# A new order for the second group of an MLP projection: three products ahead of the sums, and the sums left to VectorE

## What is computed

```python
def sqrelu_mlp(u, w1, w2):
    return jnp.square(jax.nn.relu(u @ w1)) @ w2

h = h + sliding_window_attention(rmsnorm(h, mix_norm_g), ...)
h = h + sqrelu_mlp(rmsnorm(h, mlp_norm_g), m_w1, m_w2)
gate = jax.nn.sigmoid(rmsnorm(h, ple_norm_g) @ ple_w_gate)
h = h + gate * (p @ ple_w_proj)
```

## Time and profile before

| | |
|---|---|
| median of 3 runs | 1142.06 us (1140.66 to 1142.89) |
| the profiled execution | 1143.35 us |
| its span on the core | 1141.6 us |
| PE busy | 1107.6 us, 97% of the span |
| DVE busy | 765.5 us, 67% |
| ACT busy | 453.7 us, 40% |
| POOL busy | 252.9 us, 22% |

### The profile page before, as it was taken

One profiled execution on the slowest core, in us unless ns is written; L12 is line 12 of the kernel. 1 busy time (PEld: TensorE's weight loads), 2 busy tenths in 40 slices (PEclk: granted clock), 3 DMA queues, 4 the chain that ended last, 5 costly groups with the idle time before them and its releaser, 6 DMA issues.

```text
span 1141.6 us, 15063 instructions
## 1 busy us (share of the span) xinstructions
PE 1107.6 (97%) x5418; PEld 930.1 (81%) x5418; DVE 765.5 (67%) x1129; ACT 453.7 (40%) x796; POOL 252.9 (22%) x230
## 2 busy tenths in 40 slices
PE   7899999998999996999999999999999999999998
PEld 6788888886888885888888888888888888888887
DVE  5788887888553588766766676668777774564321
ACT  5565666566432314233223323553333332243100
POOL 6532322323100185324532450000000000010000
PEclk9999999999999998999999999999999999999999
DMA  7000000013142404332533234899888882111211
GB/s 277 20 19 20 18 18 18 18 34 151 38 153 87 148 19 166 148 145 114 203 148 144 115 133 144 340 408 345 286 293 289 291 287 77 38 37 56 84 40 44
DMA packets 61801, 154.41 MB, mean 135 GB/s; under 512 B 5040, under 2 KB 6064, under 8 KB 61744
## 3 DMA queue, kind: packets, MB, share of 16 engines
q1 hardware_dynamic: 61600, 153.12, 37.4%
q10 hardware_dynamic: 144, 0.52, 0.1%
HBM read 119.55 MB, written 34.08 MB: 135 GB/s over the span
## 4 chain that ended last, share of the span: by engine, by line
PE 80%; DVE 10%; POOL 3%; ACT 3%; issue 3%; DMA 0%; ACTq 0%; DVEq 0%; POOLq 0%
PE pair L1997 23%; PE pair L1976 23%; PE pair L2040 8%; PE pair L1859 6%; PE pair L1731 5%; PE pair L2017 4%; ACT probs L895 2%; PE pair L1799 2%; PE pair L2053 2%; PE pair L1770 2%; DVE probs L1298 2%; DVE probs L1316 1%; PE pair L1936 1%; PE pair L1906 1%; PE pair L1782 1%
## 5 line engine op out<-in xcount | busy, mean ns | idle before, releaser
L1997 PE MATMUL pair<-uT 128*128 128x512 f32 x1176 | 266.7, 389 | 0.0
L1997 PEld LDWEIGHTS pair<-uT 128*128 128x128 f32 x1176 | 220.7, 188 | 45.8
L1126 ACT ACTIVATE uT<-wo_raw 128x1024 fp32r<-128x1024 f32 x63 | 63.9, 1053 | 105.0 <-PE pair L1997 89.4
L638 POOL TENSOR_SCALAR row_var<-row_ssq 128x1 f32<-128x1 f32 x24 | 4.6, 192 | 437.0 <-ACT hn L1023 430.3
L1572 DVE TENSOR_TENSOR uT<-wo_raw,uT 128x1024 fp32r<-128x1024 f32 x63 | 74.8, 1221 | 39.5 <-ACT uT L1126 39.5
L1731 PE MATMUL pair<-WA,xT 128*128 128x512 f32 x384 | 96.4, 401 | 1.4 <-DVE kn L1255 1.0
L1859 PE MATMUL pair<-WA,oT 128*128 128x512 f32 x384 | 91.6, 396 | 2.3 <-DVE WA L1374 1.7
L1859 PEld LDWEIGHTS pair<-WA,oT 128*128 128x128 f32 x384 | 72.4, 191 | 17.6 <-issue 1.9
L1731 PEld LDWEIGHTS pair<-WA,xT 128*128 128x128 f32 x384 | 70.7, 191 | 17.4 <-issue 2.9
L895 ACT ACTIVATE probs<-probs,nmax 128x257 f32<-128x257 f32 x128 | 63.7, 500 | 52.3 <-DVE nmax L1303 52.1
L1976 PE MATMUL pair<-WA,WB 128*128 128x512 f32 x312 | 74.4, 396 | 3.6 <-ACT xr L1101 3.6
(11 more groups left out here) (182 smaller groups left out, 2074.7 us busy)
## 6 DMA issues: line engine op xcount, KB each, us to landing
wo_raw<-in_m_w SPq DMA_DIRECT2D x53, 512.0 KB, 6.5
wo_raw<-hid_kept SPq DMA_DIRECT2D x36, 512.0 KB, 4.6
hid_kept<-RES SPq DMA_DIRECT2D x28, 512.0 KB, 2.6
emb<-in_m_w SPq DMA_DIRECT2D x20, 512.0 KB, 6.5
RES<-in_m_w SPq DMA_DIRECT2D x8, 1024.0 KB, 6.7
RES<-in_a_wqkv SPq DMA_DIRECT2D x12, 512.0 KB, 8.8
uT_f<-in_m_w SPq DMA_DIRECT2D x6, 1024.0 KB, 6.7
act_buf<-hid_kept SPq DMA_DIRECT2D x11, 512.0 KB, 4.6
```

The costliest lines, as they stand in the source:

```text
L1126: nc.scalar.activation(operand(t, which, HI), unit(t, which), ACT.Copy).then_inc(op_hi, 1)
L1997: mm = nc.tensor.matmul(ps[4 * (j % 2) + m][:], operand(t, 0, s)[:, k, m * P:(m + 1) * P], operand(t, 1, r)[:, k, :], start=(g == 0 and k ...
```

## The change

In group 1 alone the products now stand in the order 0, 5, 3, 1, 2, 4, 6 (`FIRST_ORDER`). The first three have quadrants of `uT` as right operands. Product 3 opens a chain of its own in `pair[3]`, so z12 is joined from two places, by two additions (`z12_part`). DVE forms all four T sums; POOL no longer forms any. Three S sums of group 1, the left operand of product 3 among them, are formed in group 0 in buffers of other tensors (`early_sums`); S1 and S2 are formed again later, in their usual places. POOL's joins of group 0 have a new order, m2, m6, m5, m1, m7, and wait for the early sums. ACT splits a left operand before it takes a partial sum in group 1, and splits T3 and T4 behind the copy of z11.

```diff
+FIRST_ORDER = (0, 5, 3, 1, 2, 4, 6)
...
         def group_of(q):
-            return q // N1 + 1, q % N1
+            return q // N1 + 1, FIRST_ORDER[q] if q < N1 else q % N1
...
+        def joined_after(q):
+            g, i = group_of(q)
+            if g == 1:
+                return {5: ("z11", 1), 2: ("z12", 2), 4: ("z22", 3), 6: ("z21", 4)}.get(i, (None, 0))
+            return {3: ("z12", 1), 4: ("z22", 2), 5: ("z11", 3), 6: ("z21", 4)}.get(i, (None, 0))
...
-            pool.wait_ge(wo_half, 2 * NB)
-            pool.wait_ge(uT_ready, 2 * NB)
-            pool.tensor_tensor(WA_f[:, T4, HI], u(LO, 0, 1), u(LO, 0, 0), ALU.subtract).then_inc(t_low, 1)
-            pool.tensor_tensor(tsum[T3], u(LO, 1, 1), u(LO, 0, 1), ALU.subtract).then_inc(t3_step, 1)
-            pool.wait_ge(t3_step, 1)
-            pool.tensor_tensor(tsum[T3], tsum[T3], u(HI, 1, 1), ALU.add).then_inc(t3_step, 1)
-            pool.wait_ge(t3_step, 2)
-            pool.tensor_tensor(tsum[T3], tsum[T3], u(HI, 0, 1), ALU.subtract).then_inc(t3_step, 1)
...
-            pool.wait_ge(z_squared, 4)
-            pool.wait_ge(hn_ready, NB)
-            join("m5", 0)
             pool.wait_ge(z_squared, 8)
-            pool.wait_ge(row_moved[7], row_kept(7))
-            join("m1", 0)
-            pool.wait_ge(uT_done, 2 * NB)
+            pool.wait_ge(a_sum, summed_by(1, 3))
             join("m2", 0)
             join("m6", 0)
+            join("m5", 0)
+
+            pool.wait_ge(a_ready, 3)
+            join("m1", 0)
             join("m7", 0)
...
             for q in range(NP):
+                if q < N1:
+                    a_hi_part(q + 2)
                 if q > 0:
                     take(q - 1)
-                if q == 0:
-                    t_hi_part(T4)
+                if N1 <= q < NP - 2:
+                    a_hi_part(q + 2)
                 if q == 1:
                     t_hi_part(T3)
-                if q + 2 < NP:
-                    a_hi_part(q + 2)
+                    t_hi_part(T4)
...
                 if i == 2:
                     t1_first()
+                    t1_second()
                 if i == 3:
-                    t1_second()
+                    t1_third()
                     t2_first()
                 if i == 4:
                     t2_second()
                     t_lo_part(T1)
                 if i == 5:
-                    a_sum_part(1)
-                    t4_first()
+                    early_sums()
                 if i == 6:
                     a_lo_part(0)
+                    a_lo_part(1)
+                    t3_first()
+                if i == 7:
+                    t4_first()
                     t_lo_part(T2)
-            a_sum_part(2)
-            a_lo_part(1)
-            t4_second()
             for q in range(NP):
                 if q > 0:
                     join_chains(q - 1)
...
                 if q == 0:
-                    a_sum_part(3)
-                    t_lo_part(T4)
+                    a_sum_part(1, 1)
+                    a_sum_part(1, 2)
+                    t3_second()
+                    t4_second()
                 if q == 1:
                     t_lo_part(T3)
+                    a_sum_part(1, 4)
+                if q == 1:
+                    t_lo_part(T4)
...
-                if i in (2, 3, 4):
+                if i in (2, 4) or (i == 3 and g > 1):
                     pe.wait_ge(z_copied, 3 * (g - 1) + i - 1)
...
                 if i == 6:
-                    pe.wait_ge(z_added, 3 * (g - 1) + 2)
-                chain = {1: pair[0], 3: pair[0], 5: pair[1]}.get(i, pair[2 if g % 2 == 1 else 3])
+                    pe.wait_ge(z_added, 3 * (g - 1) + (3 if g == 1 else 2))
+                chain = {1: pair[0], 3: pair[3] if g == 1 else pair[0], 5: pair[1]}.get(i, pair[2 if g % 2 == 1 else 3])
```

More of the change, by code:

```diff
@@ L226, in a_source @@
         def a_source(g, i):
-            sums = (first_sum if g == 1 else sum_a, sum_b, sum_a, sum_b)
+            sums = (sum_a, sum_b, early_s4, sum_c) if g == 1 else (sum_a, sum_b, sum_a, sum_b)
             return {0: lambda: w1_quadrant(g, 0, 0), 1: lambda: sums[0], 2: lambda: sums[1], 3: lambda: sums[2],
@@ L531, in _ @@
             sp.wait_ge(z_ready, 8)
-            sp.wait_ge(t_step, 1)
-            sp.wait_ge(t_low, 1)
-            sp.wait_ge(t3_step, 3)
+            sp.wait_ge(t_sum, 1)
             load_w1(2)
-            for m in ("m1", "m2", "m6", "m7"):
+            for m in ("m2", "m6", "m5", "m1", "m7"):
                 sp.wait_ge(m_ready[m], 1)
@@ L788, in _ @@
                 done = 4 * (g - 1)
-                pool.wait_ge(zq_ready, done + 2)
+                pool.wait_ge(zq_ready, done + (3 if g == 1 else 2))
                 join("m2", g)
@@ L1076, in a_hi_part @@
                 else:
[L1077 removed]
+                    act.wait_ge(a_sum, summed_by(g, i))
                 if q == 0:
@@ L1541, in join_chains @@
                 y, z, x = pair[2 if g % 2 == 1 else 3], pair[0], pair[1]
-                if i == 6:
+                buf = halves(z_buf[name])
+                if name == "z21":
                     dve.wait_ge(z_clipped, g)
-                    z21 = halves(z_buf["z21"])
-                    nc.vector.tensor_tensor(z21, y[:], z21, ALU.mult).then_inc(zq_ready, 1)
-                else:
-                    dve.wait_ge(z_copied, 3 * g)
-                    chain, name = {3: (z, "z12"), 4: (y, "z22"), 5: (x, "z11")}[i]
-                    buf = halves(z_buf[name])
-                    nc.vector.tensor_tensor(buf, chain[:], buf, ALU.add).then_inc(z_added, 1)
+                    nc.vector.tensor_tensor(buf, y[:], buf, ALU.mult).then_inc(zq_ready, 1)
+                    return
+                dve.wait_ge(z_copied, 3 * (g - 1) + {"z11": 1, "z22": 2, "z12": 3}[name])
+                chain = {"z12": z, "z22": y, "z11": x}[name]
+                if g == 1 and name == "z12":
+                    nc.vector.tensor_tensor(buf, pair[3][:], buf, ALU.add).then_inc(z12_part, 1)
+                    dve.wait_ge(z12_part, 1)
+                nc.vector.tensor_tensor(buf, chain[:], buf, ALU.add).then_inc(z_added, 1)
             def square_joined(q):
                 g, i = group_of(q)
-                if i not in (3, 4, 5):
+                name, place = joined_after(q)
+                if name in (None, "z21"):
                     return
-                dve.wait_ge(z_added, 3 * (g - 1) + i - 2)
-                buf = z_buf[{3: "z12", 4: "z22", 5: "z11"}[i]]
+                dve.wait_ge(z_added, 3 * (g - 1) + place)
+                buf = z_buf[name]
                 nc.vector.scalar_tensor_tensor(out=buf, in0=buf, scalar=0.0, in1=buf, op0=ALU.max,
@@ L1963, in product @@
                 if i == 1:
-                    wait(pe, z_added, 3 * (g - 2) + 1)
-                if i in (2, 3, 4):
+                    wait(pe, z_added, 3 * (g - 2) + (2 if g == 2 else 1))
+                if i in (2, 4) or (i == 3 and g > 1):
                     pe.wait_ge(z_copied, 3 * (g - 1) + i - 1)
@@ L1979, in product @@
                 mm.then_inc(prod_done, 1)
-            for g in range(1, NG):
-                for i in range(N1):
-                    product(g, i)
+            for q in range(NP):
+                product(q)
             def contract(t):
```

84 lines of the change are left out of this document (45 added, 39 removed).

## The result

| | before | after |
|---|---|---|
| median | 1141.95 us (22 runs, 1140.66 to 1143.14) | 1143.80 us (22 runs, 1143.19 to 1144.46) |
| ratio | | 1.0015, interval 1.0009 to 1.0021 |
| group 1, from its first product (or when it was due) to group 2 | 51.66 us | 53.28 us |

The change costs 1.85 us by the medians, 1.0 to 2.4 by the interval. That is a real difference, and under the 2.3 us that the prediction called the limit of what runs can tell. Each is read from the one profiled execution of its kernel.

The account below looks back on a forecast made before the run. PE, busy 97% of the span, bounds the kernel; only group 1 can gain. −13.58 + 7.46 + 1.84 + 2.82 + 1.73 + 1.37 + 1.65 = +3.29 us on median 1142.06 gives 1145.3; range 1140.8 to 1149.0.

Parts of the forecast that it names:

- rival 1: Group 1: POOL gets in after the T4 step, then alternates with DVE; fourth operand 9.1 late; +1.5 us, chance 0.22.
- the likeliest case: Group 1: POOL first stands back for three DVE operations, then takes turns; +3.29 us, chance 0.40 together with rival 2.
- four pieces: Group 1 before: product 0 6.23 late, then 1.84 slower; product 2 3.78 late, then 1.73 slower; all removed.
- POOL stood back for three operations, so I take that: After group 0's last square: POOL's first join gets in between S1 and S2; fourth product 7.46 us late.
- rival 2: Group 1: POOL shut out until DVE idles; fourth operand in time, fifth waits 13.1; +4.4 us, chance 0.40 with the forecast.
- The prices per turn: DVE beside POOL: a 1024 operation costs 1.09 us, a 2048 one 2.14, a join 2.27, one after another.
- The clock at the fourth product: Group 1: the wait ahead of the fourth product slows PE's clock, +1.84 us.
- The fifth product: Group 1: operand ready at 462.95, about 463 in any order; product 2.82 us late, then +1.73 for the clock.
- HI of T3 behind the copy of z11: ACT, group 1: T3's HI part follows the z11 copy, to 454.77; T3's LO part needs it.
- The structural gaps: Group 1: product six waits 1.37 us for the copy of z12, product seven 1.65 for DVE's addition of z22.
- rival 3: Group 1's last two products: short gaps slow the clock too, one or both at 1.73; +5.0 to +6.8 us, chance 0.15.
- Rival 4, joins cost DVE nothing: Group 1: POOL's and DVE's operations overlap, loss 4.0 instead of 13.58; −9.6 us, chance 0.15 with parts of it.

Follow-up runs that it names:

- the run with the T sums alone: Kernel before with only the T sums moved from POOL to DVE, product order and joins as before: 1139.90 us, ratio 0.9981.
- the run in the order of due times: Changed kernel with DVE's and ACT's work listed by when each product needs it, early sums and T steps moved to earlier pieces: 1137.19 us, ratio 0.9958.
- The run with held joins: Changed kernel with POOL's joins of group 0 held until the LO part of the fourth operand is done: 1147.48 us, ratio 1.0048.
- its two variants: Kernel before with join m2 ahead of m1 (1143.12 us, 1 run), and kernel before with only the T sums moved to DVE (1139.90 us).

## Why the prediction was right, and which step of it was not

The time was 1143.8 for 1145.3 predicted, well within a range of 8.2 us, and it moved the way that the forecast had. That it came so close is in part luck: two errors of 4.08 and 2.10 us had opposite signs. And what happened is rival 1, strict turns from the start, forecast at +1.5 and measured at +1.62 in group 1, and not the likeliest case at +3.29.

- **What the change removes** (13.58 us in four pieces): right, though the run with the T sums alone shows that the first two pieces go with POOL's sums and need no new product order. The first two products follow group 0 at once, and in the run in the order of due times five products in a row were on time. The added work in group 0 cost nothing: 38.00 busy of 38.00.
- **The failed step** is "*POOL stood back for three operations, so I take that*". POOL got in after one. The row that it rests on was weaker than it was taken for: it shows POOL let in when DVE ran out of work, not a count of three. Hence five joins, not four, ended ahead of the LO part of the fourth operand, though the fourth product waits for none of them. The fourth product lost 0.64 + 8.92 = 9.56 against 7.46; rival 1 had 9.1. The run with held joins shows the other end, +5.45 for +4.4 in rival 2: its fifth product was 13.68 late for 13.1, and the slow clock then cost 7.79 − 5.60 = 2.2 for 1.84. The prices per turn themselves (1.09, 2.14, 2.27) were right.
- **The clock at the fourth product**: its row is 7.49 where an undisturbed one is 5.60, so 1.89 for +1.84. The same event cost 1.5 to 3.0 us in other runs (rows of 7.07 to 8.59), so it has no single price.
- **The fifth product**, 2.82 late with +1.73 of clock: did not occur. As rival 1 had it, the later fourth product covers it: 2.36 − 1.89 = 0.47 for 0.4. Its operand was done at 461.20 + 1.62 = 462.8, for 463 in any order; the sum of work that must come first was right.
- **"HI of T3 behind the copy of z11"** is not on the path: that HI part waited for DVE, 4.4 us after the copy.
- **The structural gaps**: 1.50 and 1.69 for 1.37 and 1.65, at full clock; right but for 0.17, and rival 3 (short gaps slow the clock) is excluded for waits of 1.2 and 1.4; with the 0.09 at the end that makes 0.26.
- **Rival 4, joins cost DVE nothing**: its mechanism is false, five rows of 3.3 to 4.5 us show it; its price was right, since without the joins the kernel takes 1132.72, 9.3 below before, for −9.6.

So the forecast over-counted by 3.29 − 1.62 = 1.67 us: at the fifth product 4.55 − 0.47 = 4.08 too much, against 2.10 too little at the fourth, 0.05 on its clock and 0.26 on the gaps. The Trainium skill's rule in "SBUF — State Buffer", section "Who interferes with whom", that issue order decides who blocks, fits here: POOL's join at 429.17 got its turn at 431.28 (its end, 433.55, less 2.27), behind the one DVE operation issued before it, at 429.01. It does not fit the row at 438.25 of the kernel before, nor the same place in its two variants. I gave one row of the old sequence more weight than the rule; neither alone settles it.

## What to carry to other kernels

When two engines exclude each other, as DVE and POOL do here, count all their work that must come before the first operand that both serve, joins that nobody waits for too: moving a product forward frees it only if that sum gets smaller. Removing one wait then moves the loss to the next product, and here each repair showed the next late step in some queue; the first new order for DVE and ACT gave 4.8 us, and 10 came only when the orders of DVE, ACT and POOL had been put right together, by when each result is needed. A forecast that hangs on who goes first wants both orders worked out in full; here they were 1.8 us apart and the true one was the first rival.

## What the hardware showed

- **The turn is not always given by arrival.** A GpSimd join with two SBUF inputs stood back for three VectorE operations at one place of a code sequence (6.67, 6.66, 6.66 us in three kernels), until VectorE idled, and for one operation at another place of the same kernel (4.38) and in another sequence (4.38, 3.31, 4.37). From variant to variant it repeats at its place.
- **Two engines' work adds up.** Five joins of 2.27 us beside 13.4 us of VectorE work ended at 453.39, where the plain sum gives 453.7.
- **TensorE's clock.** Waits of 1.2 and 1.4 us left the product behind them at 5.7; in these groups every wait of 2.43 or more brought it down (7.32 after 2.43, 7.35 after 2.90, 7.31 after 2.96). A product behind such a wait took 7.1 to 8.6 us with no plain relation to the wait's length (7.07 after 4.58, 8.59 after 2.72, 7.79 after 13.52; 7.44 and 8.36 after 6.07 and 6.06). So the wait that shrank from 2.96 to 0.66 us in group 2 gave back 42.90 − 39.10 = 3.8 us of that group.
